# Sample attention of a hybrid decoder step: pages turned in 32x32 blocks on VectorE, scores as nine sets of four 32-row products, exponentials written to the keys' partitions

## What is computed

```
c_all  = concatenate([cache_kv[pt].reshape(L, KV_LORA), cn], 0)
kp_all = concatenate([cache_kpe[pt].reshape(L, QK_ROPE), kn], 0)
ki_all = concatenate([cache_kinv[pt].reshape(L, MLA_HEADS), sn], 0)
s = einsum('thr,kr->htk', ql, c_all) + einsum('thr,kr->htk', qp, kp_all)
s = s * ki_all.T[:, None, :] * SCALE
s = where(allowed[None], s, -inf)
p = softmax(s, axis=-1)
o_lat = einsum('htk,kr->thr', p, c_all)
```

## Time and profile before

| | us |
|---|---|
| median of 3 runs | 1609.51 |
| these runs | 1609.12 to 1610.91 |
| the profiled execution | 1610.4 |
| its span, first to last instruction | 1608.5 |
| PE busy in the span | 1558.9 (97%) |
| DVE busy | 753.2 (47%) |
| ACT busy | 587.2 (37%) |

### The profile page before, as it was taken

How to read it: one execution, slowest core, us unless ns; L and a number is a source line. 1 busy time by engine, 2 the same in 40 slices (tenths; PEclk the granted TensorE clock), 3 DMA queues, 4 the chain that set the end, 5 groups by cost and what they waited for, 6 DMA issues and landing times.

```text
span 1608.5 us, 35404 instructions
## 1 busy us (share of the span) xinstructions
PE 1558.9 (97%) x14238; PEld 1154.4 (72%) x14238; DVE 753.2 (47%) x1628; ACT 587.2 (37%) x1412; POOL 237.9 (15%) x304
## 2 busy tenths in 40 slices
PE   6999999999999999998999999999999999999998
PEld 4455566678888888876777777777767677777753
DVE  2154444457444444446565656657565623013422
ACT  3056444454333333253535444363535231210000
POOL 0000230310122212010000000000000025536200
PEclk9999999999999999999999999999999999999999
DMA  9713787712444444421111111111111125343302
GB/s 328 269 53 113 223 229 262 187 49 84 111 116 119 118 118 120 113 57 29 35 51 41 39 41 38 41 52 40 51 29 49 29 55 176 80 140 96 112 4 82
DMA packets 179518, 159.95 MB, mean 99 GB/s; under 512 B 37866, under 2 KB 157674, under 8 KB 178332
## 3 DMA queue, kind: packets, MB, share of 16 engines
q1 hardware_dynamic: 168780, 118.46, 25.6%
q0 software_dynamic: 9648, 36.19, 7.3%
q10 hardware_dynamic: 928, 3.05, 0.5%
HBM read 133.02 MB, written 24.64 MB: 98 GB/s over the span
## 4 chain that ended last, share of the span: by engine, by line
PE 67%; DVE 5%; ACT 4%; DVEq 2%; issue 1%; POOL 0%; ACTq 0%
PE me_bank L2838 12%; PE rw_bank L1653 9%; PE sa_psS L1120 8%; PE sa_psOs L1148 7%; PE me_bank L2858 3%; PE sa_psA L1105 3%; PE rw_bank L1692 2%; DVE rw_gram L2415 2%; PE sa_psS L1117 2%; PE rw_bank L1754 1%; PE rw_bank L1665 1%; PE rw_bank L1678 1%; PE rw_bank L1773 1%; PE rw_bank L1905 1%; PE rw_bank L1825 1%
## 5 line engine op out<-in xcount | busy, mean ns | idle before, releaser
L1653 PE MATMUL rw_bank<-hT,big 128*128 128x288 f32 x672 | 183.0, 417 | 0.8 <-ACT prep L2090 0.7
L1653 PEld LDWEIGHTS rw_bank<-hT,big 128*128 128x128 f32 x672 | 122.0, 190 | 33.1 <-issue 2.3
L1120 PE MATMUL sa_psS<-qlT,sa_cT_pages 128*128 128x128 f32 x1024 | 131.3, 282 | 0.0
L1120 PEld LDWEIGHTS sa_psS<-qlT,sa_cT_pages 128*128 128x128 f32 x1024 | 119.1, 192 | 7.7
L1215 ACT COPY sa_cT_pages<-sa_psA 128x512 f32<-128x512 f32 x128 | 68.7, 589 | 145.7 <-PE sa_psA L1105 145.7
L1262 DVE TENSOR_TENSOR sa_ST<-sa_psS,kinvp 128x512 f32<-128x512 f32 x64 | 44.3, 692 | 151.5 <-PE sa_psS L1120 150.9
L1678 PE MATMUL rw_bank<-hT,big 128*128 128x288 f32 x256 | 73.5, 421 | 0.0
L739 PE MATMUL pr_psZ<-hT,qlT 128*128 128x288 f32 x256 | 73.1, 406 | 0.1
L1451 POOL COPY shc<-prep 128x3 f32<-128x3 f32 x8 | 1.5, 188 | 470.7 <-ACT rw_xs L2118 470.7
L993 POOL DMA_DIRECT2D big<-in_cache_kv x80 | 44.2, 552 | 180.1 <-issue 180.1
L2897 ACT COPY big<-me_bank 128x288 f32<-128x288 f32 x42 | 16.7, 398 | 144.8 <-PE me_bank L2838 141.7
(11 more groups left out here) (541 smaller groups left out, 3247.9 us busy)
## 6 DMA issues: line engine op xcount, KB each, us to landing
big<-in_w_in SPq DMA_DIRECT2D x44, 512.0 KB, 4.2
big<-in_cache_kv POOLq DMA_DIRECT2D x80, 128.0 KB, 2.9
pages<-in_cache_kv POOLq DMA_DIRECT2D x80, 128.0 KB, 2.7
fr_wada<-in_w_ada SPq DMA_DIRECT2D x8, 1024.0 KB, 11.6
qk_scratch<-oaT SPq DMA_DIRECT2D x32, 192.0 KB, 2.6
big<-in_cache_kv SPq DMA_DIRECT2D x48, 128.0 KB, 2.7
pages<-in_cache_kv SPq DMA_DIRECT2D x48, 128.0 KB, 2.7
fr_wada<-in_w_ada SPq DMA_DIRECT2D x2, 2048.0 KB, 10.3
```

Source lines behind the costliest of these rows:

```text
L1120: last = nc.tensor.matmul(psS[:, c, 0:ROW], cT[:, g % 2, r, c * P:(c + 1) * P], M.qlT[:, r, n, :, :].rearrange("p h t -> p (h t)"), start= ...
L1653: last = mm(bank[h][:, 0:HT], w[:, ORDER[q], k, :], M.hT[:, k, (F0, F1)[h]], start=(k == 0), stop=(k == KT - 1))
```

## The change

- **Turning.** The transposes on PE and the copies on ACT go. DVE turns a group's 128 keys x 4 pages x 256 latents by one instruction (`latents_by_blocks`, `v.transpose`) that transposes each 32x32 block within its own 32 partitions. So `cT` holds, in each 32 partitions, 32 latent rows of 32-key blocks.
- **Loading.** A page is spread so that 32 of its keys lie in each quarter of the partitions; still one DMA for each page, with the four page numbers read ahead of the four DMAs. SP takes five of eight groups (it was four), POOL three.
- **Scores.** Nine sets of four products over 32 rows: one for the rotary part, eight for the latents. The queries have to stand in each quarter of the partitions (`q4`), in blocks of 32 latent rows. They are written once to a scratch in DRAM (`q_dram`) and loaded for each sample by four DMAs.
- **Exponentials.** A result now stands in other partitions than its latents. `exponentials` writes to the keys' partitions: 16 instructions on 32 partitions for each of five chunks, into a ring of six places (`weights`), four for the last sample. Chunks are of 1, 1, 2, 2, 2 groups, as before in size.
- **Order.** `LAG` is 3. `output(n - 2)` moves on DVE from step g = 0 to the end of step g = 2. The own tokens' centring has its own semaphore. The calls for the last sample in `rwkv` are spread otherwise.

```diff
 def _load_group(e, I, M, s, g, landed):
-    for q in (0, 2, 1, 3) if g % 2 == 0 else (2, 0, 3, 1):
-        at = s * PAGES + GP * g + q
-        page = e.value_load(M.table[0:1, at:at + 1], min_val=0, max_val=M.n_phys - 1)
-        src = I["cache_kv"][bass.ds(page, 1), :, :].rearrange("a (k c) n -> (a k) c n", c=GP)
-        e.dma_start(M.pages[s % 2][q * QP:(q + 1) * QP, g, :, 0:KL], src).then_inc(landed, 16)
+    at = s * PAGES + GP * g
+    listed = [e.value_load(M.table[0:1, at + c:at + c + 1], min_val=0, max_val=M.n_phys - 1) for c in range(GP)]
+    for c, page in enumerate(listed):
+        src = I["cache_kv"][bass.ds(page, 1), :, :].rearrange("a (j b) n -> (a b) j n", b=GP)
+        e.dma_start(M.pages[s % 2][:, g, c, 0:KL], src).then_inc(landed, 16)
...
-        LAG = 2
+        LAG = 3
...
             sp.wait_ge(M.absorb_tr, 3)
             sp.dma_start(own, I["own_mask"]).then_inc(own_in, 16)
+            sp.wait_ge(M.absorb_ev, 4)
+            store_queries(slice(0, 1), q_out)
+            sp.wait_ge(q_out, 16 * GP)
+            load_queries(0)
+            store_queries(slice(1, BD), q_out)
...
             def scores(n, g):
...
-                for c in range(GP):
-                    for r in range(2):
-                        last = nc.tensor.matmul(psS[:, c, 0:ROW], cT[:, g % 2, r, c * P:(c + 1) * P], M.qlT[:, r, n, :, :].rearrange("p h t -> p (h t)"),
-                                                start=False, stop=(r == 1))
+                for a in range(NCB):
+                    for b in range(GP):
+                        rows = rows_of(b)
+                        last = nc.tensor.matmul(psS[:, b, 0:ROW], cT[rows, g % 2, a, :], q4[n % 2][rows, a, :], start=False, stop=(a == NCB - 1))
                 last.then_inc(scored, 1)
...
+                ring, n = place(s, a)
+                for k in range(GP):
+                    for j in range(GP):
+                        got = STs[s % 2][rows_of(k), GP * a + j:GP * b:GP, :]
+                        done = nc.scalar.activation(ring[rows_of(j), n:n + b - a, k, :], got, ACT.Exp, scale=SCALE)
+                done.then_inc(exped, 1)
...
+            def latents_by_blocks(n, g):
+                wait_pages(dve, n, g)
+                if G * n + g >= 2:
+                    dve.wait_ge(scored, G * n + g - 1)
+                got = M.pages[n % 2][:, g, :, 0:KL].rearrange("p c (a i) -> p c a i", i=ROPE)
+                v.transpose(cT[:, g % 2, :, :].rearrange("p a (c j) -> p c a j", j=QP), got).then_inc(cT_sb, 1)
...
             for n in range(BD):
                 for g in range(G):
                     weighted_scores(n, g)
+                    ahead = G * n + g + 2
+                    if ahead < G * BD:
+                        latents_by_blocks(ahead // G, ahead % G)
...
+                    if n >= 2 and g == LAG - 1:
+                        output(n - 2)
```

More of the change, by code:

```diff
@@ L1027, in sample @@
+        centred, own_centred, exped, pv, o_sb, o_tr, o_T, up, gated = (
+            sem(n) for n in ("centred", "own_centred", "exped", "pv", "o_sb", "o_tr", "o_T", "up", "gated"))
         block, last = M.block, Shared()
         M.last_sample = last
-        last.pv, last.weighted, last.topped, last.cT_sb, last.up, last.gated = pv, weighted, topped, cT_sb, up, gated
+        last.pv, last.weighted, last.topped, last.kT_sb, last.up, last.gated = pv, weighted, topped, kT_sb, up, gated
+        rows_of = lambda n: slice(n * ROPE, (n + 1) * ROPE)
@@ L1031, in wait_pages @@
+        place = lambda s, g: (weights, (G * s + g) % PLACES) if s + 1 < BD else (last_weights, g % LAST_PLACES)
         def wait_pages(e, n, g):
-            if n < 2:
-                e.wait_ge(M.pages_in[n % 2][g], 16 * GP)
-            elif g % 2 == 1:
+            if n >= 2 and g in BY_SP:
+                e.wait_ge(pages_in[g], 16 * GP * (n - 1))
+            else:
                 e.wait_ge(M.pages_in[n % 2][g], 16 * GP * (n // 2 + 1))
-            else:
-                e.wait_ge(pages_in[n % 2][g // 2], 16 * GP * (n // 2))
@@ L1126, in own_tokens @@
                     pe.wait_ge(top_taken, n)
+                else:
+                    pe.wait_ge(M.absorb_ev, 4)
+                    pe.wait_ge(M.o_sb, NP)
                 if n > 1:
@@ L1179, in _ @@
                         top_to_columns(n - 1)
-                    if n + 1 < BD and g + 1 == G:
-                        transposes(n + 1, 0)
                     scores(n, g)
@@ L1233, in _ @@
             for n in range(BD):
[L1234 to L1246 removed]
+                if n == 0:
+                    for hp in range(2, NP):
+                        M.gate_sigmoid(act, hp)
+                else:
+                    exponentials(n - 1, 0)
+                    exponentials(n - 1, 1)
+                    if n >= 2:
+                        output_to_sbuf(n - 2)
+                    exponentials(n - 1, 2)
+                    exponentials(n - 1, 3)
+                if n + 1 < BD:
+                    keys_to_sbuf(n + 1)
+                if n > 0:
+                    exponentials(n - 1, 4)
             last.exponentials, last.output_to_sbuf = exponentials, output_to_sbuf
@@ L2247, in _ @@
             tail.output_to_sbuf(BD - 2)
-            for c in range(2, tail.chunks):
-                tail.exponentials(BD - 1, c)
+            tail.exponentials(BD - 1, 2)
             act.wait_ge(tail.pv, G * (BD - 1))
@@ L2259, in _ @@
             projected(0, 0, 0)
+            tail.exponentials(BD - 1, 3)
             projected(0, 0, 1)
@@ L2262, in _ @@
             gates(0)
+            tail.exponentials(BD - 1, 4)
             key_factor(0)
@@ L2547, in _ @@
             tail.spread_top(BD - 1)
-            tail.centre(BD - 1, 0)
+            for c in range(3):
+                tail.centre(BD - 1, c)
+            tail.own_centre(BD - 1)
             tail.output(BD - 2)
-            tail.centre(BD - 1, 1)
             dve.wait_ge(M.oa_stored, 16)
@@ L2554, in _ @@
             vectors()
-            for c in range(2, tail.chunks):
+            for c in range(3, tail.chunks):
                 tail.centre(BD - 1, c)
```

210 lines of the change are left out of this document (108 added, 102 removed).

## The result

The changed kernel takes **1654.21 us** (median of 4 runs, 1653.92 to 1655.05) against 1610.21 for the kernel before on the same chip; ratio 1.0275, 95% interval 1.0257 to 1.0292. Predicted were 1651, with a range of 1612 to 1676.

What follows compares the result with a forecast made beforehand. PE, busy 97% of the span, was taken as the bound. Terms 7.5 + 4.0 + 1.0 - 4.5 + 0 + 14.5 + 19 for the clock = +41.5 on 1610.4 gave 1651.9, by the runs' median 1651 us; range 1612 to 1676.

Steps and rivals of the forecast that it cites:

- start, to the first reading: First scores wait for the queries' way through DRAM, 8.7 us: +7.5 us, bounds +5 to +12; clock 2 more.
- samples 2 to 6: Steady samples take 42.1 us instead of 43.0, PE losing 5.8 of 7.0 saved to two waits: -4.5, clock 2.5 each.
- tail: Behind the last reading ScalarE becomes the bound through the new exponentials: +14.5 us; +3 if overlapping, +19 with more table loads.
- A set of four products at 0.22: Scores on PE: four 32-row products overlap fully and cost one latent product, 0.22 us; a step is 4.15.
- The rival of partly overlapping sets: Scores on PE: a set costs between 0.22 and 0.43, say 0.30 us, giving 1686 us; chance 10%.
- A transposition at 1.25: VectorE's turning of a group, 1024 elements in a partition, was taken at 1.25 us, at most 2.5.
- The rival of 2.5: VectorE's transposition costs double, +1.25 us each in PE's waits and the first sample's steps: 1675 us; chance 6%.
- Exponentials at 0.31 and 0.43: ScalarE's 32-partition exponentials don't overlap: 4.9 us for a one-group chunk, 6.8 for two, 30.4 a sample.
- The wait for `o_sb` at 4.8: At step 3 PE stands 4.8 us before `latents_to_columns`, until VectorE has made the quotient.
- The rival that VectorE would not hold TensorE: At step 3, six waits of 3.8 us and the clock's drops would go: 1603 us; chance 13%.
- The clock: PE's clock halves behind long pauses: 2.5 us for each of six, 2 each for start and second sample; +19, bounds 0 and +27.
- That the clock holds: Drops of PE's clock need more than these pauses: +22.5, so 1632 us; chance 18%.

Runs made afterwards that it cites:

- Experiment 4: Changed kernel with the last sample's exponentials as five wide 128-partition instructions instead of eighty, landing on the wrong partitions: 1638.35 us.
- experiment 3: Changed kernel with 40 unused transpositions on TensorE just before its wait for `o_sb` in six samples: 1651.73 us.
- experiment 7: Kernel of experiment 1 with group 7's pages of each later sample loaded by GpSimd's queue and not SyncE's: 1629.90 us.
- experiments 5 and 6: Changed kernel with the first sample's queries loaded early from another tensor (1643.81 us), or made by copies between partitions on ScalarE and VectorE (1645.32 us).
- experiment 1: Changed kernel with the quotient of the sample before last made one step earlier on VectorE, before its turning of the pages: 1646.48 us.
- experiment 10: Kernel of experiment 7 with exponentials in four chunks of two groups instead of five, 64 instructions a sample instead of 80: 1619.91 us.

## Why the prediction was right, and where it was not

| term | predicted | measured |
|---|---|---|
| start, to the first reading | +7.5 and 2 for the clock | 354.1 to 364.2: +10.1 |
| first sample | +4.0 | 25.8 to 29.1: +3.4 |
| second sample | +1.0 and 2 | 40.5 to 41.7: +1.2 |
| samples 2 to 6 | -4.5 and 5 x 2.5 | 215.0 to 226.4: +11.4 |
| last sample | 0 and 2.5 | 41.3 to 43.0: +1.7 |
| tail | +14.5 | 931.8 to 948.2: +16.4 |
| sum | +41.5 | span 1608.5 to 1652.6: +44.1 |

- **A set of four products at 0.22.** The weight loads of eight sets take 1.88 us where the clock is full (L1145; 1.86 for eight full-height products), and a step without waits 4.15 or 4.16. The rival of partly overlapping sets is out. The figure of 3.07 in the Trainium skill ("TensorE: Matmul & The Clock Gate", Part 3) is for 512 columns; with 128 columns this trace shows four products at the price of one.
- **A transposition at 1.25:** 64 of them, 1.24 each. The rival of 2.5 is out. (That rival's sum names three places in a sample and counts two.)
- **Exponentials at 0.31 and 0.43, one behind the other:** 0.31 and 0.41, 16 in 5.1 and 6.8 us. As forecast, ScalarE didn't hold TensorE in samples 2 to 6. Experiment 4 shows by taking them away that in the tail they cost what was said; the form with 128 partitions brought back 14.2 of 16.4.
- **The wait for `o_sb` at 4.8:** 4.5 us idle for the products and 4.7 for their weight loads, where nothing else was late, with the steps at 4.9, 5.5, 4.8 and 11.7 for 4.9, 5.7, 4.75 and 9.25 + 2.5. The rival that VectorE would not hold TensorE is out.
- **The clock:** a drop to half at each stall, as said; experiment 3 prices it at 2.8 us in a steady sample and 2.5 on average of the six, for 2.5. That the clock holds is out. But the prediction tied the drops to the long pauses, and shorter ones are followed by them too: 1.39 us at the start, 2.03 in three samples of experiment 7.
- **The start:** 7.35 us idle instead of 8 to 9; experiments 5 and 6 take 10.4 and 8.9 away. TensorE begins its first scores 8.3 us later than before (359.84 for 351.55) for the 7.5 reckoned, and takes 1.8 more for them at half clock, for 2. The term is known to some 3 us only: eight traces with the same start have their first reading between 362.1 and 368.0.
- **The tail:** ScalarE leaves the chain 60.2 us behind the last reading, for 61.1, which is +13.6 for +14.5. The sum had no clock there, and that is what it lacks: TensorE then waits 4.23 us at L1186 where it waited 1.30, and its next sixteen products take 5.41 us at half clock, 4.05 before. That makes 15.0 of the 16.4; the rest was not traced.

What the prediction missed is that the stall is not alone. It reckoned each wait as if nothing stood behind it, and said nothing of SyncE. Its sum for the samples holds, but not as a price for the cure: taking the stall away brings 8 us and not 42, and its faster rival, for which these waits go, was put at 1603 where experiment 1 gives 1646, since SyncE's issuing (about 39 us a sample, with the four query loads and 20 page loads) and the five chunks of exponentials stand close behind. This was argued from the rows and then shown by experiments 7 (only another queue: 16.6 us) and 10 (only 16 instructions a sample fewer: 10.0 by the medians, 7.4 in the samples). Samples 2 to 4 took 44.3 us each, for 44.6; samples 5 and 6 took 4.9 more than these, with their waits for pages. Why SyncE falls behind only there is not settled.

There is luck in the total, too. Without the stall and its drops the kernel would have taken 1646, with the stall and with TensorE kept busy in it 1652, and both lie within 5 us of the forecast 1651, as the measured 1654 does. What bears the prediction out is not the sum but its single steps: the wait at its place, the clock behind it, and the steps of samples 2 to 4.

So the term that was mis-sized is that of samples 2 to 6, +11.4 for +8.0, since SyncE's load was not counted; the tail is off by +1.9, and the other four by -2.7 together, which is why the sum came out at 2.6 from the measured one. (The prediction says that TensorE gives 5.8 of the 7.0 us saved to its two waits; by its own 42.1 for 43.0 it gives 6.1.)

## What to carry to other kernels

A wait that an edit adds must be priced with the next bound behind it: list for one period what each engine and each issuing queue is busy for, since removing the visible stall gains only down to the next of them. Where an instruction's output moves to other partitions, count instructions, not elements, and look where the engine that runs them has a stage's critical chain; the same moves were dear on ScalarE, and dearer on VectorE ahead of a quotient (a tail of 952.3 us, 947.8 in experiment 10). In VectorE's gaps they went with a tail of 940.3, but three other edits were made with them there. And expect late data to take back what a fuller clock gives: 15.0 us in the steps of experiment 3 became 2.5 in its median. A datum that only changes partitions (here 128 rows, 1 KB in each) is cheaper by copies on idle engines than by a round trip over DRAM: 3.7 us against 9.

## What the runs showed of the hardware

- Four products over 32 rows and 128 columns, each in its own row division, cost together what one over 128 rows costs: weight loads of 64 instructions in 1.88 us, of 16 in 1.86 in the kernel before.
- Instructions on 32 partitions that go to another quarter of the partitions each time don't overlap on ScalarE: 32 of 128 elements in 10.20 us, 16 of 256 in 6.78. On VectorE 16 subtractions of 32x256 take 6.86 us, 0.43 each. No run has such instructions in one and the same quarter, so whether it is the width or the change of quarter is open.
- A stall of 4.2 to 5.1 us on TensorE came each time with 3.4 or 6.8 us of half clock, which begins late in the stall or within a microsecond behind it and falls for the most part on the work behind it; keeping TensorE at work on dummy transpositions prevented it. Of five waits of 2.03 us (experiment 7) three were followed by a fall, and one of 1.39 us at the start.
- Issuing a DMA took SyncE 0.5 to 0.7 us when its queue was calm; behind page loads a query load took 1.2 to 2.1 us, a page load 0.7 to 1.7. A page load on GpSimd's queue took 0.67.
